# Rotations and squares of the last attention mixer on GpSimd, its values evacuated by VectorE, the exponential's table loaded early

## The chip, the cores and the metric

The program runs on one core of one Trainium2 chip. A core has TensorE (matrix products, called PE in the profile), VectorE (DVE), ScalarE (ACT), GpSimd (POOL) and SyncE (SP, which here only issues the transfers). Every engine works through its own list of instructions in order; semaphores tie the lists together. The metric is the time of one execution on the device in microseconds (us), and of several executions the median.

## What is computed

Two blocks of a transformer on 256 positions of width 1024, batch 1, all in float32. The first block has a recurrent layer, a sparse attention and a feed-forward part. The second has two layers, each with a feed-forward part, a mixer and another feed-forward part. The mixer of its second layer, the odd mixer, is what most of the change touches:

```python
proj = rmsnorm(x, od_norm) @ od_w_in
c_q, c_kv, k_pe, gq, gk, gv = split(proj)          # 256, 128, 32, 512, 128, 128 columns
q = (rmsnorm(c_q, od_cq_norm) @ od_w_uq)           # 8 heads of 64 + 32
kv = (rmsnorm(c_kv, od_ckv_norm) @ od_w_ukv)       # 8 heads of 64 (keys) + 64 (values)
k = concat(k_nope, k_pe for all heads)
q, k = rmsnorm(q), rmsnorm(k); the last 32 columns of a head are rotated (rope)
out_c = gqa_attention(q, k, v_c)                   # 8 heads, called D in the kernel
qd, kd = axial_rope(rmsnorm(gq)), axial_rope(rmsnorm(gk))
out_d = gqa_attention(qd, kd, gv)                  # 8 query heads on 2 key heads, called C
mix = concat(out_c, out_d) @ od_w_out;  x = x + mix
```

`gqa_attention` is softmax(q k / sqrt(d)) v.

## The kernel before

**Weights.** All weights stream once through the core, in chunks of 128x1024 float32 or less (`stream`, numbered). SyncE transfers chunk i into a ring of six buffers (`RAW`); ScalarE rounds it to the fast matmul format (`hi(e, i)`, line 312, result `WH`); VectorE computes what the rounding left over (`lo(e, i)`, line 318, result `WL`, which also frees the `RAW` buffer for SyncE). TensorE then adds three products per piece of 128 input features (lines 345 to 347): high activation by high weight, high by low, low by high. Activations are split in the same way, `AT0h`/`AT0l` for the layer's input and `AT3h`/`AT3l` for the latents of the odd mixer. `dense(e, p, x0, x1)` issues passes x0 to x1 of product p; a pass is one chunk for one half of the positions.

**The odd mixer** runs on the profile from about 1124 us to 1236 us. TensorE computes OGQ and OGK (queries, keys and values of attention C) and OCQ (the latents), turns keys and latents (transposes by a matmul with the identity, line 391), and computes UKV and UQ (keys, values and queries of attention D from the latents). Then come the eight units of attention C and the eight of D. A unit is two heads on 128 query positions:

- `pe_scores` writes the scores of unit u into PSUM bank 4 or 5 (`att_s`)
- `dve_max` takes their maxima (lines 538, 541)
- `act_exp` makes the exponentials and their sums (line 557, `att_e`), which frees the bank
- `pe_turn_p` turns them into bank 6 (line 391, `SR` or `SL`); it waits for `act_exp` of its unit and `act_p` of the unit before
- `act_p` copies the turned block out (line 599), and `pe_values` multiplies with the values (line 616)

After four units `dve_out`, `pe_turn_out`, `act_out_hi` and `dve_out_lo` prepare the input of the output product (OO for C, OP for D). Since TensorE takes its list in order, other work stands between the steps of the units: passes of UKV, UQ, OO and OP.

**Before the units** each product is evacuated by ScalarE: `act_ukv` (lines 1800, 1802, 1804: keys, their squares, values), `act_uq` (lines 1811, 1812: queries, their squares). VectorE rotates in six instructions per group (`dve_odd_rot`, lines 1660 to 1671, groups gq, gk, pe, q), sums the squares (`dve_mla_sums`, line 1703), takes the roots and scales the keys. ScalarE's table of functions has to hold the exponential before line 557; what is in use before (the SiLU set of the feed-forward part) does not have it, so a table load stands ahead of the first `act_exp`.

**The order** of all engines in the mixers is written out by hand, as lists (`pe_odd_mixer`, `act_odd_mixer`, `dve_odd_mixer` and the same for the first mixer and for the norm between its feed-forward part and the second block, `pe_post_norm`, `act_post_norm`, `dve_post_norm`). GpSimd has 21 instructions in the whole program, none of them in the odd mixer but one clearing of `KG`.

## Time and profile before

| | us |
|---|---|
| median of three executions | 1427.22 |
| lowest, highest | 1423.85, 1429.24 |
| the profiled execution | 1423.9 |
| its span, first to last instruction | 1422.1 |
| TensorE busy in it | 1393.8 (98%) |
| VectorE busy | 879.7 (62%) |
| ScalarE busy | 770.7 (54%) |
| GpSimd busy | 13.0 (1%) |

The profiled execution took 1.8 us more than its span. The page also gives the clock granted to TensorE: 0.994 on average, where 1.0 is 2.4 GHz and 0.5 is 1.2 GHz, the only two levels. Busy time of TensorE contains the pipelined tail of every matmul, about 0.17 us, so a wait shorter than that is invisible and a longer one looks that much shorter. Starts of instructions are the better ruler: in steady work a 128x512 matmul starts every 0.23 us.

### The profile page before, as it was taken

What the parts mean: (1) busy time and instruction counts of PE and PEld (TensorE: products, weight loads), DVE (VectorE), ACT (ScalarE), POOL (GpSimd) and SP (SyncE); (2) the same over time, 40 slices, a digit from 0 to 9 for tenths busy, and PEclk for the clock granted to TensorE, in tenths of its full rate; (3) what the DMA queues carried; (4) which work ended last, traced back from release to release, by engine and by line L of the source; (5) the groups of instructions that cost most, each with busy time, mean ns of one, the idle gap of its engine ahead of it and who ended that gap; (6) DMA issues with size and microseconds to landing.
All of it is one profiled execution on the core that took longest, in us unless ns stands there. A gap on an engine that the chain in (4) does not pass through costs nothing.

```text
span 1422.1 us, 18520 instructions
## 1 busy us (share of the span) xinstructions
PE 1393.8 (98%) x6978; PEld 1173.7 (83%) x6978; DVE 879.7 (62%) x1345; ACT 770.7 (54%) x1169; POOL 13.0 (1%) x21
## 2 busy tenths in 40 slices
PE   7999999999999999999999999999999989999999
PEld 6799888788887888888788888888888868888887
DVE  6889846665545755557976555565555674565543
ACT  5589844554545544445765444454444576554441
POOL 2000000000000000000000000000000000000000
PEclk9999999999999999999999999999999989999999
DMA  8453556476655566566346655666655431366651
GB/s 298 142 161 106 160 166 182 144 216 184 190 180 168 187 186 185 182 189 205 113 155 196 190 180 191 183 189 180 188 182 189 145 118 59 106 212 187 191 180 60
DMA packets 131767, 242.57 MB, mean 171 GB/s; under 512 B 8544, under 2 KB 21472, under 8 KB 131680
## 3 DMA queue, kind: packets, MB, share of 16 engines
q1 hardware_dynamic: 130768, 239.15, 54.7%
q0 software_dynamic: 624, 2.10, 0.5%
q8 instruction: 57, 0.93, 0.3%
q14 instruction: 30, 0.25, 0.0%
q10 hardware_dynamic: 288, 0.14, 0.0%
HBM read 240.31 MB, written 1.05 MB: 170 GB/s over the span
## 4 chain that ended last, share of the span: by engine, by line
PE 95%; DVE 2%; ACT 2%; issue 0%; DMA 0%; SPq 0%; ACTq 0%; DVEq 0%
PE PB L345 28%; PE PB L347 27%; PE PB L346 27%; PE PB L391 5%; PE PB L616 2%; PE PB L505 2%; PE PB L339 1%; PE PB L341 1%; PE PB L340 1%; DVE WL L318 1%; PE PB L509 0%; DMA X<-in_x_dram 0%; DVE XC L783 0%; PE PB L797 0%; PE PB L986 0%
## 5 line engine op out<-in xcount | busy, mean ns | idle before, releaser
L318 DVE TENSOR_TENSOR WL<-RAW,WH 128x1024 fp32r<-128x1024 f32 (+1 forms) x453 | 548.4, 1217 | 442.4 <-ACT WH L312 440.9
L312 ACT ACTIVATE WH<-RAW 128x1024 fp32r<-128x1024 f32 (+1 forms) x453 | 475.6, 1055 | 517.2 <-PE PB L347 509.0
L345 PE MATMUL PB<-WH,AT0h 128*128 128x512 f32 (+3 forms) x1328 | 507.9, 382 | 6.6 <-DVE AT0l L1232 6.5
L347 PE MATMUL PB<-WH,AT0l 128*128 128x512 f32 (+3 forms) x1328 | 497.6, 375 | 0.0
L346 PE MATMUL PB<-WL,AT0h 128*128 128x512 f32 (+3 forms) x1328 | 497.0, 374 | 0.0
L345 PEld LDWEIGHTS PB<-WH,AT0h 128*128 128x128 f32 x1328 | 250.9, 189 | 51.6 <-issue 10.1
L347 PEld LDWEIGHTS PB<-WH,AT0l 128*128 128x128 f32 x1328 | 250.7, 189 | 44.7
L346 PEld LDWEIGHTS PB<-WL,AT0h 128*128 128x128 f32 x1328 | 251.2, 189 | 44.1 <-issue 2.2
L345 PE MATMUL PB<-WH,FTh 128*128 128x512 f32 x440 | 172.1, 391 | 0.0
L347 PE MATMUL PB<-WH,FTl 128*128 128x512 f32 x440 | 171.3, 389 | 0.0
L346 PE MATMUL PB<-WL,FTh 128*128 128x512 f32 x440 | 171.2, 389 | 0.0
L347 PEld LDWEIGHTS PB<-WH,FTl 128*128 128x128 f32 x440 | 82.6, 188 | 17.3
L346 PEld LDWEIGHTS PB<-WL,FTh 128*128 128x128 f32 x440 | 82.7, 188 | 16.8
L345 PEld LDWEIGHTS PB<-WH,FTh 128*128 128x128 f32 x440 | 82.6, 188 | 16.8
L1280 ACT ACTIVATE SR<-PB,SM 128x512 f32<-128x512 f32 (+1 forms) x60 | 38.7, 653 | 24.7 <-PE PB L347 24.6
L391 PE MATMUL PB<-ID,SR 128*128 128x128 f32 x316 | 45.2, 277 | 5.2 <-ACT SR L557 5.0
L391 PEld LDWEIGHTS PB<-ID,SR 128*128 128x128 f32 x316 | 37.6, 144 | 12.3 <-ACT SR L557 5.5
L1309 ACT ACTIVATE FTh<-PB 128x512 fp32r<-128x512 f32 x55 | 30.2, 596 | 21.3 <-PE PB L391 21.3
L1287 DVE SCALAR_TENSOR_TENSOR SR<-PB,SM,SR 128x512 f32<-128x512 f32 (+1 forms) x60 | 39.9, 700 | 0.5
L339 PE MATMUL PB<-AT0h,WH 128*128 128x256 f32 x128 | 39.6, 309 | 0.0
L1315 DVE TENSOR_TENSOR FTl<-PB,FTh 128x512 fp32r<-128x512 f32 x55 | 35.6, 686 | 2.4 <-ACT FTh L1309 0.3
L341 PE MATMUL PB<-AT0h,WL 128*128 128x256 f32 x128 | 36.1, 282 | 0.0
(304 smaller groups left out, 1043.0 us busy)
## 6 DMA issues: line engine op xcount, KB each, us to landing
RAW<-in_ffn_w_gu_dram SPq DMA_DIRECT2D x88, 512.0 KB, 4.0
RAW<-in_ffn_w_gu_2b_dram SPq DMA_DIRECT2D x88, 512.0 KB, 3.7
RAW<-in_w_in_dram SPq DMA_DIRECT2D x48, 512.0 KB, 4.1
RAW<-in_ffn_w_down_dram SPq DMA_DIRECT2D x44, 512.0 KB, 3.3
RAW<-in_ffn_w_down_2b_dram SPq DMA_DIRECT2D x44, 512.0 KB, 3.3
RAW<-in_w_ffn_gate_dram SPq DMA_DIRECT2D x22, 512.0 KB, 4.0
RAW<-in_w_ffn_up_dram SPq DMA_DIRECT2D x22, 512.0 KB, 3.7
RAW<-in_w_ffn_down_dram SPq DMA_DIRECT2D x22, 512.0 KB, 3.6
```

What stands on the lines that cost most here:

```text
L312: e.activation(WH[i % NHL][:, 0:m], RAW[i % NRAW][:, 0:m], ACT.Copy).then_inc(*up("hi", i))
L318: e.tensor_tensor(WL[i % NHL][:, 0:m], RAW[i % NRAW][:, 0:m], WH[i % NHL][:, 0:m].bitcast(F32), ALU.subtract).then_inc(*up("lo", i))
L339: e.matmul(o, h[:, f], p.src[0][:, kx, :], start=start, stop=False, skip_group_check=True)
L341: ins = e.matmul(o, l[:, f], p.src[0][:, kx, :], start=False, stop=stop, skip_group_check=True)
L345: e.matmul(o, p.src[0][:, kx, t], h[:, j:j + p.n], start=start, stop=False)
L346: e.matmul(o, p.src[0][:, kx, t], l[:, j:j + p.n], start=False, stop=False)
L347: ins = e.matmul(o, p.src[1][:, kx, t], h[:, j:j + p.n], start=False, stop=stop)
L391: ins = e.transpose(PB[bank][0:s.shape[1], j * 128:j * 128 + 128], s, ID[:, :])
L1280: e.activation(silu_out(f, g, b), PB[p.banks[b]][:, 0:p.n], ACT.Silu, scale=RS[f"f{f}"][:, b:b + 1]).then_inc(*up("f_silu", (f, g, b)))
L1287: e.scalar_tensor_tensor(sl, PB[p.banks[b]][:, 0:p.n], RS[f"f{f}"][:, b:b + 1], sl, ALU.mult, ALU.mult).then_inc(*up("f_mult", (f, g, b)))
L1309: e.activation(FT[0][:, t:t + 2, :].rearrange("p t s -> p (t s)"), PB[4 + 2 * (g % 2) + q][:, :], ACT.Copy).then_inc(*up("f_hi", (f, g, q)))
L1315: e.tensor_tensor(FT[1][:, t:t + 2, :].rearrange("p t s -> p (t s)"), PB[4 + 2 * (g % 2) + q][:, :], FT[0][:, t:t + 2, :].rearrange("p t s ...
```

## The change

1. In the odd mixer the four rotations go from VectorE to GpSimd, 24 instructions (`pool_odd_rot`). They count on a semaphore of their own (`rot`).
2. The squares of keys and queries, eight instructions, go from ScalarE (out of PSUM) to GpSimd (out of the evacuated copies, `pool_uk_square`, `pool_uq_square`).
3. The values are evacuated by VectorE (`dve_uv`) instead of ScalarE, after ScalarE has read the same bank.
4. Of the squares of the latents, the second half of the positions goes from ScalarE to VectorE (`dve_cq_square`).
5. `act_warm`, one exponential of a 128x1 tile, stands behind the input of the odd mixer. The table load goes with it.
6. The lists of all engines are written in another order, in the odd mixer, in the first mixer and in the norm before the second block. Products, sizes and the stream of weights are the same.

```diff
@@ -1649,26 +1649,34 @@
                     "gk": [OUT3[:, :, 512 + z * 64:576 + z * 64].rearrange("p b (h d) -> p b h d", h=2) for z in range(2)],
                     "pe": [KT3[:, 2 * z:2 * z + 2, 0:16].unsqueeze(2) for z in range(2)]}
 
-        def dve_odd_rot(e, name, part):
+        def pool_odd_rot(e, name, part):
             x, h, half, tabs, i = ROT[name]
             x1, x2 = x[:, :, :, 0:half], x[:, :, :, half:2 * half]
             tmp = ROT_ROOM[name]
             tab = lambda j: tabs[:, i, j].unsqueeze(2).broadcast_to([128, 2, h, half])
             if part == 0:
                 e.wait_ge(*on(*ROT_FROM[name]))
-                e.wait_ge(*(on("heads", ("gq", 2)) if name == "q" else on("tab", "o")))
-                e.tensor_tensor(tmp[0], x1, tab(0), ALU.mult).then_inc(*up("dve"))
-                e.tensor_tensor(tmp[1], x2, tab(1), ALU.mult).then_inc(*up("heads", (name, 0)))
+                e.wait_ge(*(on("rot", ("gq", 2)) if name == "q" else on("tab", "o")))
+                e.tensor_tensor(tmp[0], x1, tab(0), ALU.mult).then_inc(*up("rot"))
+                e.tensor_tensor(tmp[1], x2, tab(1), ALU.mult).then_inc(*up("rot", (name, 0)))
             elif part == 1:
-                e.wait_ge(*on("heads", (name, 0)))
+                e.wait_ge(*on("rot", (name, 0)))
                 if name == "pe":
-                    e.wait_ge(*on("jk", ("cq", 1, 2)))
-                e.tensor_tensor(x1, x1, tab(2), ALU.mult).then_inc(*up("dve"))
-                e.tensor_tensor(x2, x2, tab(3), ALU.mult).then_inc(*up("heads", (name, 1)))
+                    e.wait_ge(*on("jk", ("cq", 2)))
+                    e.wait_ge(*on("cqs", 2))
+                e.tensor_tensor(x1, x1, tab(2), ALU.mult).then_inc(*up("rot"))
+                e.tensor_tensor(x2, x2, tab(3), ALU.mult).then_inc(*up("rot", (name, 1)))
             else:
-                e.wait_ge(*on("heads", (name, 1)))
-                e.tensor_tensor(x1, x1, tmp[1], ALU.subtract).then_inc(*up("dve"))
-                e.tensor_tensor(x2, x2, tmp[0], ALU.add).then_inc(*up("heads", (name, 2)))
+                e.wait_ge(*on("rot", (name, 1)))
+                e.tensor_tensor(x1, x1, tmp[1], ALU.subtract).then_inc(*up("rot"))
...
@@ -1698,12 +1706,13 @@
 
             v = v_m[:, 16 * i:16 * i + 16]
             v3 = v.rearrange("p (b h) -> p b h", b=2)
-            e.wait_ge(*on("evac", (("uks1", "uqs1")[i], 1)))
+            e.wait_ge(*on("usq", ("kq"[i], 1, 1)))
             sq = SQ3[:, :, 512 * i:512 + 768 * i].rearrange("p b (h d) -> p b h d", h=8)
             e.tensor_reduce(v3, sq, AXX, ALU.add).then_inc(*up("dve"))
             e.wait_ge(*last("dve"))
             if i == 0:
-                e.wait_ge(*on("jk", ("cq", 1, 2)))
+                e.wait_ge(*on("jk", ("cq", 2)))
+                e.wait_ge(*on("cqs", 2))
                 e.scalar_tensor_tensor(v3, v3, 96 * EPS, ssp.unsqueeze(2).broadcast_to([128, 2, 8]), ALU.add,
                                        ALU.add).then_inc(*up("heads", ("v", "k")))
             else:
...
+            q_ready=[("rot", ("q", 2))], k_ready=[("mkT", 3)], v_ready=[("uv", (1, 1))], q_first=1,
             bank6=[("att_p", ("c", 7))], bank45={0: [("att_e", ("c", 6))], 1: [("att_e", ("c", 7))]},
             bank7={0: [("o_lo", ("c", 1))], 1: [("o_lo", ("d", 0))]},
             slot_free={u: [("att_tp", ("c", u + 2))] for u in range(6)},
@@ -1778,15 +1787,26 @@
                 e.scalar_tensor_tensor(AT3[1][:, t, :], PB[6 + q][:, i * S:i * S + S], col("cq", t),
                                        AT3[0][:, t, :].bitcast(F32), ALU.mult, ALU.subtract).then_inc(*up("cq_lo", t))
 
-        def act_cq_square(e, b):
-            e.wait_ge(*on("evac", ("cq", b)))
+        CQ_PARTS = ((0, 256), (256, 128), (384, 32))
+
+        def act_cq_square(e):
+
+            e.wait_ge(*on("evac", ("cq", 0)))
             e.wait_ge(*last("jk"))
-            cond_square(e, JK[:, 0, 0:256], CQ[:, b, 0:256], ssc[:, b:b + 1], ("cq", b, 0))
-            cond_square(e, JK[:, 1, 0:128], CQ[:, b, 256:384], ssc[:, 2 + b:3 + b], ("cq", b, 1))
-            cond_square(e, JK[:, 1, 128:160], CQ[:, b, 384:416], ssp[:, b:b + 1], ("cq", b, 2))
+            for i, (o, n) in enumerate(CQ_PARTS):
+                t = (ssc[:, 0:1], ssc[:, 2:3], ssp[:, 0:1])[i]
+                cond_square(e, JK[:, 0, o:o + n], CQ[:, 0, o:o + n], t, ("cq", i))
+
+        def dve_cq_square(e):
+            e.wait_ge(*on("evac", ("cq", 1)))
+            for i, (o, n) in enumerate(CQ_PARTS):
+                x, t = CQ[:, 1, o:o + n], (ssc[:, 1:2], ssc[:, 3:4], ssp[:, 1:2])[i]
+                e.scalar_tensor_tensor(JK[:, 1, o:o + n], x, 1.0, x, ALU.mult, ALU.mult,
+                                       accum_out=t).then_inc(*up("cqs", i))
 
         def dve_cq_root(e):
-            e.wait_ge(*on("jk", ("cq", 1, 2)))
+            e.wait_ge(*on("jk", ("cq", 2)))
+            e.wait_ge(*on("cqs", 2))
             e.tensor_scalar(ssc[:, 0:2], ssc[:, 0:2], 0.5, 128 * EPS, ALU.mult, ALU.add).then_inc(*up("dve"))
             e.tensor_scalar(ssc[:, 2:4], ssc[:, 2:4], 128 * EPS, None, ALU.add).then_inc(*up("dve"))
...
@@ -1799,24 +1819,35 @@
             e.wait_ge(*on("rc", "rc"))
             e.activation(kh[:, b, 4 * c:4 * c + 4, 0:64], x[:, :, 0:64], ACT.Copy,
                          scale=s).then_inc(*up("evac", (f"uk{c}", b)))
-            e.activation(SQ3[:, b, c * 256:c * 256 + 256].rearrange("p (h d) -> p h d", d=64), x[:, :, 0:64], ACT.Square,
-                         scale=s).then_inc(*up("evac", (f"uks{c}", b)))
-            e.activation(V3[:, b, c * 256:c * 256 + 256].rearrange("p (h d) -> p h d", d=64), x[:, :, 64:128], ACT.Copy,
-                         scale=s).then_inc(*up("evac", (f"uv{c}", b)))
+        def dve_uv(e, c, b):
+            x = PB[UKV[c].banks[b]][:, :].rearrange("p (h d) -> p h d", d=128)
+            e.wait_ge(*on("evac", (f"uk{c}", b)))
+            e.tensor_scalar(V3[:, b, c * 256:c * 256 + 256].rearrange("p (h d) -> p h d", d=64), x[:, :, 64:128],
+                            ysc[:, 2 + b:3 + b], None, ALU.mult).then_inc(*up("uv", (c, b)))
+
+        def pool_uk_square(e, c, b):
+            x = kh[:, b, 4 * c:4 * c + 4, 0:64]
+            e.wait_ge(*on("evac", (f"uk{c}", b)))
+            e.tensor_tensor(SQ3[:, b, c * 256:c * 256 + 256].rearrange("p (h d) -> p h d", d=64), x, x,
+                            ALU.mult).then_inc(*up("usq", ("k", c, b)))
+
+        def pool_uq_square(e, c, b):
+            n = UQ[c].n
+            x = Q3[:, b, 512 * c:512 * c + n]
+            e.wait_ge(*on("evac", (f"uq{c}", b)))
+            e.tensor_tensor(SQ3[:, b, 512 + 512 * c:512 + 512 * c + n], x, x, ALU.mult).then_inc(*up("usq", ("q", c, b)))
 
         def act_uq(e, c, b):
             p, s = UQ[c], ysc[:, b:b + 1]
             x = PB[p.banks[b]][:, 0:p.n]
             e.wait_ge(*on("mm", p.end(b)))
             e.activation(Q3[:, b, 512 * c:512 * c + p.n], x, ACT.Copy, scale=s).then_inc(*up("evac", (f"uq{c}", b)))
-            e.activation(SQ3[:, b, 512 + 512 * c:512 + 512 * c + p.n], x, ACT.Square,
-                         scale=s).then_inc(*up("evac", (f"uqs{c}", b)))
...
@@ -2269,11 +2295,11 @@
             pe_scores(e, AT_C, 1)
             dense(e, UKV[1], 1, 2)
             dense(e, UQ[0], 0, 2)
-            dense(e, UQ[1], 0, 2)
             pe_turn_p(e, AT_C, 0)
             pe_scores(e, AT_C, 2)
+            dense(e, UQ[1], 0, 2)
+            pe_turn_p(e, AT_C, 1)
             pe_scores(e, AT_C, 3)
-            pe_turn_p(e, AT_C, 1)
             pe_values(e, AT_C, 0)
             pe_turn_q(e, AT_C, 1)
             pe_values(e, AT_C, 1)
@@ -2281,66 +2307,64 @@
             pe_scores(e, AT_C, 4)
             pe_scores(e, AT_C, 5)
             pe_turn_p(e, AT_C, 3)
+            pe_values(e, AT_C, 2)
+            pe_values(e, AT_C, 3)
+            pe_turn_p(e, AT_C, 4)
+            pe_scores(e, AT_C, 6)
+            pe_scores(e, AT_C, 7)
...
@@ -2678,6 +2702,7 @@
             hi(e, 371)
             act_x_hi(e, 'od', 2)
             act_x_hi(e, 'od', 3)
+            act_warm(e)
             hi(e, 372)
             hi(e, 373)
             act_gq(e, 0)
...
+            act_cq(e, 1)
             act_keys3(e, 0)
-            act_keys3(e, 1)
-            act_cq(e, 1)
-            act_cq_square(e, 0)
             act_cq_hi(e, 0)
             act_cq_hi(e, 1)
-            act_cq_square(e, 1)
+            act_keys3(e, 1)
+            hi(e, 380)
             act_q(e, AT_C, 0)
-            hi(e, 380)
             hi(e, 381)
             act_ukv(e, 0, 0)
             act_ukv(e, 0, 1)
             act_ukv(e, 1, 0)
             act_ukv(e, 1, 1)
+            hi(e, 382)
+            act_exp(e, AT_C, 0)
             act_uq(e, 0, 0)
             act_uq(e, 0, 1)
-            act_uq(e, 1, 0)
-            act_uq(e, 1, 1)
-            act_exp(e, AT_C, 0)
             act_exp(e, AT_C, 1)
             act_p(e, AT_C, 0)
-            hi(e, 382)
+            act_uq(e, 1, 0)
             hi(e, 383)
+            act_uq(e, 1, 1)
+            act_exp(e, AT_C, 2)
             act_p(e, AT_C, 1)
-            act_exp(e, AT_C, 2)
+            act_exp(e, AT_C, 3)
             act_q(e, AT_C, 1)
-            act_exp(e, AT_C, 3)
+            hi(e, 384)
             act_p(e, AT_C, 2)
-            hi(e, 384)
...
@@ -2780,31 +2804,31 @@
         def dve_first_mixer(e):
             lo(e, 0)
             lo(e, 1)
+            lo(e, 2)
             dve_in_lo(e, 0)
             dve_in_lo(e, 1)
             dve_in_lo(e, 2)
-            dve_in_lo(e, 3)
-            lo(e, 2)
             lo(e, 3)
             lo(e, 4)
+            dve_in_lo(e, 3)
             lo(e, 5)
...
-            dve_post_root(e, 'f1', 1)
+            lo(e, 143)
             dve_block_lo(e, 'f1', 0, 0)
             dve_block_lo(e, 'f1', 0, 1)
+            dve_post_root(e, 'f1', 1)
+            lo(e, 144)
             dve_post(e, 'f1', 1, 0)
             dve_post(e, 'f1', 1, 1)
-            lo(e, 143)
-            lo(e, 144)
             dve_block_lo(e, 'f1', 1, 0)
+            dve_rs(e, 'f1')
             dve_block_lo(e, 'f1', 1, 1)
-            dve_rs(e, 'f1')
...
             lo(e, 374)
-            dve_odd_rot(e, 'gq', 2)
             lo(e, 375)
-            dve_odd_rot(e, 'gk', 0)
             dve_gqa_sums(e)
-            dve_odd_rot(e, 'gk', 1)
+            lo(e, 376)
             dve_gqa_root(e)
-            dve_odd_rot(e, 'gk', 2)
-            lo(e, 376)
-            dve_gqa_keys(e)
             lo(e, 377)
             lo(e, 378)
+            dve_gqa_keys(e)
             lo(e, 379)
-            dve_odd_rot(e, 'pe', 0)
+            dve_cq_square(e)
             dve_cq_lo(e, 0)
             dve_cq_lo(e, 1)
             dve_cq_root(e)
-            dve_odd_rot(e, 'pe', 1)
+            lo(e, 380)
+            dve_uv(e, 0, 0)
+            dve_uv(e, 0, 1)
+            dve_uv(e, 1, 0)
             dve_max(e, AT_C, 0)
+            dve_uv(e, 1, 1)
             dve_max(e, AT_C, 1)
-            lo(e, 380)
-            dve_odd_rot(e, 'pe', 2)
+            dve_mla_sums(e, 0)
             lo(e, 381)
-            dve_mla_sums(e, 0)
-            dve_odd_rot(e, 'q', 0)
+            dve_max(e, AT_C, 2)
+            lo(e, 382)
+            dve_max(e, AT_C, 3)
             dve_mla_sums(e, 1)
...
@@ -3185,6 +3202,28 @@
             lo(e, 393)
             lo(e, 394)
             lo(e, 395)
...
```

The order at three places. The first is VectorE at the start of the program: `GR` is the normed input, line 444 makes `AT0l`, which the first product waits for.

```order
 L422 TENSOR_SCALAR GR<-X,SM 128x512 x4
-L318 TENSOR_TENSOR WL<-RAW,WH 128x1024 x2
-L444 SCALAR_TENSOR_TENSOR AT0l<-PB,CO,AT0h 128x256 x8
-L318 TENSOR_TENSOR WL<-RAW,WH 128x1024 x2
+L318 TENSOR_TENSOR WL<-RAW,WH 128x1024 x3
+L444 SCALAR_TENSOR_TENSOR AT0l<-PB,CO,AT0h 128x256 x6
+L318 TENSOR_TENSOR WL<-RAW,WH 128x1024
 L318 TENSOR_TENSOR WL<-RAW,WH 128x576
+L444 SCALAR_TENSOR_TENSOR AT0l<-PB,CO,AT0h 128x256 x2
 L318 TENSOR_TENSOR WL<-RAW,WH 128x1024
```

A third weight chunk now stands ahead of the first `AT0l`. The second place is VectorE in the norm before the second block, where lines 359 to 376 with 128x1 operands are the root of the second half of the positions.

```order
 L1195 TENSOR_TENSOR X<-SR,X 128x512
-L318 TENSOR_TENSOR WL<-RAW,WH 128x1024
+L318 TENSOR_TENSOR WL<-RAW,WH 128x1024 x2
+L1232 SCALAR_TENSOR_TENSOR AT0l<-PB,CO,AT0h 128x128 x8
 L1181 SCALAR_TENSOR_TENSOR SM<-SM 128x1
 L359 TENSOR_SCALAR SM<-SM 128x1
```

The eight instructions that make `AT0l` moved ahead of that root, and one more weight chunk ahead of them. The third place is ScalarE in the odd mixer, from the last squares of the keys to the second unit of attention C, first of before:

```order
L1804 ACTIVATE V<-PB,SM 128x256
L1811 ACTIVATE Q<-PB,SM 128x512
L1812 ACTIVATE SQ<-PB,SM 128x512
L1811 ACTIVATE Q<-PB,SM 128x512
L1812 ACTIVATE SQ<-PB,SM 128x512
L1811 ACTIVATE Q<-PB,SM 128x256
L1812 ACTIVATE SQ<-PB,SM 128x256
L1811 ACTIVATE Q<-PB,SM 128x256
L1812 ACTIVATE SQ<-PB,SM 128x256
L557 ACT_TABLE_LOAD
L557 ACTIVATE SR,SM<-PB,SM 128x256 x4
```

and of the change, from the keys on (line 1820 is `act_ukv`, 1844 is `act_uq`):

```order
L1820 ACTIVATE K<-PB,SM 128x4x64 x4
L312 ACTIVATE WH<-RAW 128x1024
L557 ACTIVATE SR,SM<-PB,SM 128x256 x2
L1844 ACTIVATE Q<-PB,SM 128x512 x2
L557 ACTIVATE SR,SM<-PB,SM 128x256 x2
L599 ACTIVATE PT<-PB 128x512
L1844 ACTIVATE Q<-PB,SM 128x256
L312 ACTIVATE WH<-RAW 128x1024
L1844 ACTIVATE Q<-PB,SM 128x256
```

The first exponential moved ahead of all evacuations of the queries; squares, values and the table load are gone from between. The table load now stands behind line 1250 at the mixer's start; the number of table loads in the program is 21 in both.

## Rows read from the trace of the kernel before

**Rows 1.** The page's first part: busy time, share of the span, instructions.
```profile
PE 1393.8 (98%) x6978; PEld 1173.7 (83%) x6978; DVE 879.7 (62%) x1345; ACT 770.7 (54%) x1169; POOL 13.0 (1%) x21
```
**Rows 2.** Waits of PE in the whole span: total us, times, longest.
```profile
PE PB L391 <- ACT SR L557: 5.0, 2, 4.4
```
**Rows 3.** Busy us of each engine, PEclk, DMA by window; window and length first.
```profile
75.00:180.00 105.00, 104.86 (x704) 94.38 (x702) 89.85 (x147) 89.40 (x181) 1.26 (x3) 1.00 0.46 139
1147.00:1161.00 14.00, 12.31 (x54) 9.32 (x52) 9.23 (x29) 12.94 (x37) 0.00 (x0) 0.88 0.45 146
1161.00:1170.00 9.00, 4.65 (x10) 2.36 (x10) 5.72 (x17) 7.97 (x17) 0.00 (x0) 0.68 0.21 63
1170.00:1188.00 18.00, 16.59 (x120) 13.98 (x120) 11.75 (x21) 14.48 (x38) 0.00 (x0) 0.97 0.28 87
1188.00:1224.00 36.00, 36.00 (x226) 31.77 (x225) 15.57 (x28) 21.49 (x52) 0.00 (x0) 1.00 0.20 60
```
**Rows 4.** Timeline of PE, odd mixer: start, duration, line, tiles, count, idle before.
```profile
1165.47 1.11 PE L391 MATMUL PB<-ID,SR 128*128 128x128 f32 x4 [4.35 <-ACT SR L557]
...
1169.79 1.06 PE L391 MATMUL PB<-ID,SR 128*128 128x128 f32 x4
...
1178.41 0.61 PE L391 MATMUL PB<-ID,SL 128*128 128x128 f32 x4
1178.86 1.00 PE L616 MATMUL PB<-G,PT 128*128 128x64 f32 x8
1179.70 1.08 PE L505 MATMUL PB<-KG,QT 128*128 128x512 f32 x2
1180.61 0.60 PE L391 MATMUL PB<-ID,SL 128*128 128x128 f32 x4
...
1192.73 0.58 PE L345 MATMUL PB<-WH,AT0h 128*128 128x512 f32 x1
```
**Rows 5.** Timeline of ACT, odd mixer.
```profile
1153.69 1.06 ACT L312 ACTIVATE WH<-RAW 128x1024 fp32r<-128x1024 f32 x1 [1.04 <-PE PB L347]
1154.65 0.46 ACT L1800 ACTIVATE K<-PB,SM 128x256 f32<-128x256 f32 x1
...
1155.36 0.47 ACT L1804 ACTIVATE V<-PB,SM 128x256 f32<-128x256 f32 x1
...
1158.93 0.77 ACT L1811 ACTIVATE Q<-PB,SM 128x512 f32<-128x512 f32 x1
1159.50 0.78 ACT L1812 ACTIVATE SQ<-PB,SM 128x512 f32<-128x512 f32 x1
...
1162.92 1.28 ACT L557 ACT_TABLE_LOAD   x1
1164.21 0.56 ACT L557 ACTIVATE SR<-PB,SM 128x256 f32<-128x256 f32 x1
...
1165.31 0.56 ACT L557 ACTIVATE SR<-PB,SM 128x256 f32<-128x256 f32 x1
```
**Rows 6.** Groups of DVE by form, 1130 to 1188 us: busy us, mean ns.
```profile
L1703 DVE TENSOR_REDUCE SM<-SQ 128x16 f32<-128x1536 f32 x1 | 1.7, 1747 | 0.0
...
L1660 DVE TENSOR_TENSOR OUT<-G,TG 128x512 f32<-128x512 f32 x1 | 0.7, 691 | 1.4 <-ACT G L1633 1.4
```
**Rows 7.** Groups of POOL by form, whole span: busy us, mean ns.
```profile
L648 POOL MEMSET IKT<- 128x512 f32 x1 | 0.5, 544 | 0.0
...
L1018 POOL TENSOR_SCALAR_AFFINE_SELECT SC<-SC 128x256 f32<-128x256 f32 x1 | 0.4, 408 | 7.3 <-DVE SC L1012 7.3
```
**Rows 8.** Timelines of DVE and PE at the start of the program.
```profile
11.16 2.35 DVE L318 TENSOR_TENSOR WL<-RAW,WH 128x1024 fp32r<-128x1024 f32 x2
13.43 3.22 DVE L444 SCALAR_TENSOR_TENSOR AT0l<-PB,CO,AT0h 128x256 fp32r<-128x256 f32 x8
...
14.05 0.47 PE L345 MATMUL PB<-WH,AT0h 128*128 128x512 f32 x1
```
**Rows 9.** Timelines of DVE and PE in the norm before the second block.
```profile
461.61 2.15 DVE L1232 SCALAR_TENSOR_TENSOR AT0l<-PB,CO,AT0h 128x128 fp32r<-128x128 f32 x8
...
462.87 0.47 PE L345 MATMUL PB<-WH,AT0h 128*128 128x512 f32 x1 [3.25 <-DVE AT0l L1232]
```

450 lines of the change are left out of this document (229 added, 221 removed).

## The prediction, made before the changed kernel ran

> **What bounds the kernel now.** I read the page's first part, then PE's waits, then the windows of the odd mixer, then the timelines there. TensorE is busy for 98% of the span [rows 1], so only what keeps it standing or at its lower clock can be given back. Its longest wait outside the start is for the first exponentials of attention C, 5.0 us in two waits, one of 4.4 [rows 2]. The windows show where the loss lies [rows 3]. From 1147 to 1188 us TensorE is not busy for 14 - 12.31 = 1.69, 9 - 4.65 = 4.35 and 18 - 16.59 = 1.41 us, together 7.45. The granted clock there is 0.88, 0.68 and 0.97, and since time at the lower level (1.2 GHz) does half the work, that is another 0.12 x 14 + 0.32 x 9 + 0.03 x 18 = 1.7 + 2.9 + 0.5 = 5.1 us. So about 12.5 us is all that the odd mixer has to give. Behind it, from 1188 to 1224, TensorE is busy in 36.00 of 36 us at full clock, and in the first mixer's dense part (75 to 180) in 104.86 of 105 us: there a new order can gain nothing and can only lose.
>
> **The ScalarE chain of the odd mixer (parts 2, 3 and 5 of the change).** Before, ScalarE runs from the first key evacuation at 1154.65 to the table load at 1162.92 without a gap. Keys, squares, values of one block take 0.36 us each (0.71 for two, 1154.65 to 1155.36), a 512 wide query block or its squares 0.57 (1158.93 to 1159.50). Then come 1.28 us of table load, and the exponentials start at 1164.21, one unit each 1.10 us (1164.21 to 1165.31) [rows 5]. TensorE turns unit 0 at 1165.47 and unit 1 at 1169.79, the latter at the lower clock [rows 4].
>
> Afterwards, walked with the same durations: the fourth key evacuation still has to wait for the last UKV pass, and ends near 1157.0. One weight chunk follows (about 1.0 us, the step from 1153.69 to 1154.65 in [rows 5]), so the exponentials of unit 0 run from 1157.9 to 1159.0. TensorE has finished the UQ[0] passes at 1159.1 and turns unit 0 at once, computes the scores of unit 2 (0.91, from 1179.70 to 1180.61) and the two UQ[1] passes (1.4), and can turn unit 1 at 1161.9; the exponentials of unit 1 end at 1161.2. That is 7.9 us ahead of 1169.79, with one scores unit less behind it: 7.0 ahead. The table load costs nothing where it goes: ScalarE is waiting for TensorE there, for about as long as the load, and the next weight chunk is needed many passes later. If that cover failed it would cost at most its 1.28 us.
>
> **What is late next.** The rest of attention C. ScalarE has per unit 1.10 us of exponentials and 0.5 of copy, TensorE 0.45 (turn), 0.84 (values) and 0.91 (scores) [rows 4]. Three short waits remain in my walk: 1.1 us where the second query turn waits for the copy of unit 1, 0.3 for that query copy, 0.7 where the exponentials of unit 4 wait for VectorE, which has the sums of the query squares (1.75 us, [rows 6]) and the root ahead of its maxima: 2.1 in all. Ahead of them the latents' chain keeps 1.3 us of its 1.69 idle, and the clock drop behind it 1.6. So 12.5 - 2.1 - 2.9 = 7.5 us are given back. A second count agrees roughly: continued to the scores of attention D, the walk puts TensorE 8.1 us ahead of where it is at 1192.73. I take **7.5 us**, with 4 and 11 as ends. Attention D keeps enough passes of OO and OP between its steps to stay full, as it is now [rows 3].
>
> **The latents (part 4).** One set of three small squares leaves ScalarE's path between the second latent evacuation and `AT3h`, and key evacuations take most of its place: 0.4 us, contained in the 7.5. It cannot exceed the 1.69 us.
>
> **GpSimd (parts 1 and 2).** The trace shows no GpSimd instruction with two inputs. The floor is the clearing of 128x512, 0.54 us; one input for 256 elements costs 0.41, so 0.82 for 512, and two inputs read in turn would be 1.64 [rows 7]. I take the middle of the last two, 1.2 us per 512, against 0.69 on VectorE [rows 6]. The rotation of the queries (6 x 1.2) and of the keys (6 x 0.3) then runs from 1133.0 to 1142.0, and the key product has to be ready at 1146.9, with 0.4 us for VectorE between. So these 9 us lie beside TensorE's OGK and OCQ passes. They stay covered up to about 1.58 us per 512; at the end of 1.64 they cost 0.4. The squares of the queries end at about 1164.1 and gate the sums named above; at 1.64 they cost about 0.9. The rotation of the D queries ends near 1168, and is needed near 1182. Nobody else waits in GpSimd's queue: its transfers are all issued earlier.
>
> The rotations' own time on VectorE disappears, but VectorE was not what TensorE waited for, so that gain is nought. The values cost VectorE four instructions of 128x256 in place of it, and the banks of UQ now come free through it; it has them done by 1157.4, before TensorE needs the second bank.
>
> The Trainium skill (GPSIMD Engine Reference, section 3.1) has GpSimd's `tensor_tensor` 1.96 times slower than VectorE's. By that, as an estimate, a 512 wide one takes 1.35 us; no run here shows it yet, and the sum would stay the same, since 1.35 is below 1.58.
>
> **The start (part 6).** VectorE now makes a third low weight chunk ahead of the first `AT0l`. Two take from 11.16 to 13.43, so one is 1.14 us; its input is ready in time. `AT0l` starts at 13.43 and TensorE's first product at 14.05 [rows 8], and TensorE has no wait of length until far behind. So the start is **1.1 us later**, with nothing to take it up; between 0.5 and 1.2, since TensorE's transposes end near 14.0 too.
>
> **The norm before the second block (part 6).** TensorE stands for 3.25 us there; `AT0l` starts at 461.61 and the product at 462.87 [rows 9], behind one weight chunk and the eight small instructions of a root. After the change two weight chunks stand ahead (1.14 more) and the root (1.65) does not: **0.5 us earlier**, between 0 and 0.8. The root then falls behind `AT0l`, under four dense passes of 1.36 us.
>
> **The first mixer (part 6).** The order moves between products, none of which is added. With 0.14 us idle in 105 it can gain nothing there; what a slip costs is a wait of the kind this trace has, 0 to 3 us. I take 0.
>
> **Sum.** -7.5 - 0.5 + 1.1 = **-6.9 us** against the profiled execution of 1423.9 (span 1422.1), so 1417.0. That execution lies 3.3 us below the median of 1427.2; the median moves by the same amount, to **1420.3**.
>
> **The rivals.**
> A, the forecast: 4.5 to 9 us gained, 1418.2 to 1422.7. Chance 0.50.
> B, the walk is too careful: the clock does not drop behind the latents, and the short waits vanish, worth up to 1.6 + 2.1, so 9 to 11 us gained, about 1417. For it: the idle stretches there become shorter. Against it: the latents' chain keeps most of its links. Chance 0.13.
> C, the clock drops once more: TensorE gets short waits, 2.1 us within 8, where before it had one long one, and a drop like the one around 1166 to 1170 costs 1.7 to 3. Gain about 4.5, 1422.7. Against it: from 1170 to 1188 it had 1.41 us of waits and stayed near 0.97. Chance 0.14.
> D, the first mixer slips: 3 us lost where VectorE and ScalarE are each busy for 89 of 105 us [rows 3]. Gain about 4, 1423.4. Chance 0.13.
> E, slower than before: GpSimd's two-input instructions are far slower than the rows suggest, and `pe_keys3` stands in TensorE's order ahead of the whole chain. Per us above 1.58 for 512 elements the two rotations end 6 x 1.25 = 7.5 us later and TensorE stands as long, and the squares add some 3 us at the sums. Above 2.3 us the gain of 6.9 is gone; at 3 us the time is 1434. The end of the rows is 1.64, which speaks against it. Chance 0.07.
> F, VectorE and GpSimd hinder one another. The Trainium skill (SBUF — State Buffer, "Who interferes with whom") says that a VectorE instruction with two SBUF inputs and a GpSimd one that reads SBUF exclude each other for the whole instruction. No row here shows it. As a mechanism of this kernel: the weight chunk ahead of the maxima of units 2 and 3 and the root are such instructions, and GpSimd has its squares and rotations at that time; each could be held for one GpSimd instruction, 0.6 to 1.2 us, two or three of them in the path. Gain about 5, 1422.3. Chance 0.03 on its own, since A's lower end holds most of it.
>
> **How the numbers follow.** The likeliest case is A, so 1420.3. B's end and the spread of the medians (1423.9 to 1429.2 before) put the low end at 1415.5; C, D, F and a median 2 us off put the high end at 1426; E is left out. What a measurement can tell from no change is about 0.5%, here 7.1 us, to 1420.1. The forecast of 6.9 lies on that bound. Faster: half of A less a little (0.23), all of B and some of the rest by the medians' spread (0.20), 0.43. Slower by over 0.5%: the worse part of E and chance, 0.06. Within 0.5%: 0.51.
>
> **What would show it.** The table load near 1126 us and none at the first exponentials; PE's wait of 4.35 us for `SR` gone, the exponentials of unit 0 near 1158, unit 1 turned near 1162; the first product at 15.1 instead of 14.05; the wait in the norm near 2.7 instead of 3.25; GpSimd's 128x512 instruction between 0.8 and 1.6 us, and no wait of PE at line 391 for the keys. It would be wrong if a wait of several us stood in the first mixer, if PEclk fell to 0.5 a second time between 1160 and 1185, or if GpSimd's squares ended long after 1164 and the maxima of unit 4 with them.

## The result, and the profile after

| | before | changed |
|---|---|---|
| median, us (20 executions each, same chip) | 1428.82 | 1422.78 |
| lowest, highest | 1423.85, 1429.53 | 1419.16, 1424.21 |
| ratio, 95% interval | | 0.9965 [0.9956, 0.9973] |
| span of the profiled execution | 1422.1 | 1421.0 |

By the ratio, in which all kernels are compared, the change gains 5.0 us (3.9 to 6.3), within the 0.5% that was called no change; the two medians differ by 6.0. Forecast were 6.9 us and 1420.3; the range holds the time.

The two profiled spans differ by only 1.1 us, the medians by more. That of before is its shortest execution (1423.9 where the median of 20 is 1428.8). Most executions of before have a mean granted clock between 0.990 and 0.993 (15 of 18 beside the first experiments), this one had 0.994. So one trace against one trace tells where waits are, and not what the clock costs on average. I keep the two apart below.

TensorE's waits over 0.15 us in the changed kernel (us in total, times, longest), against [rows 2]:

```profile
PE PB L391 <- DVE GR L422: 10.6, 1, 10.6
PE PB L345 <- DVE AT0l L1232: 6.0, 2, 3.2
PE PB L391 <- ACT SL L557: 2.3, 1, 2.3
PE PB L391 <- POOL CQ L1671: 1.3, 1, 1.3
PE PB L345 <- DVE AT0l L444: 0.9, 1, 0.9
PE PB L391 <- ACT PT L599: 0.9, 1, 0.9
PE PB L391 <- DVE G L1702: 0.5, 1, 0.5
PE PB L391 <- ACT QT L487: 0.2, 1, 0.2
```

The wait of 4.4 for `SR` is gone; of the last six, five stand in the odd mixer. (`CQ L1671` is the latents' pause. TensorE waits there to turn the queries into the bank from which `AT3h` and `AT3l` are made; the profile names GpSimd's rotation, which ended at nearly the same moment. In the kernel's list this step waits for the first `AT3l`, which ended at 1155.86, 0.15 us before TensorE's start; in rot_on_vector below, without rotations on GpSimd, the profile names `AT3l` here.) The windows of [rows 3] in the changed kernel. This execution reached the odd mixer 5.6 us later than that of before (GpSimd clears `KG` at 1126.1 instead of 1120.5), so each shows work that lies 5.6 us earlier:

```profile
1147.00:1161.00 14.00, 12.16 (x63) 10.10 (x63) 12.76 (x38) 9.82 (x22) 6.89 (x15) 1.00 0.42 151
1161.00:1170.00 9.00, 8.07 (x47) 6.24 (x46) 8.81 (x15) 8.84 (x22) 6.96 (x8) 1.00 0.39 122
1170.00:1188.00 18.00, 15.47 (x96) 12.31 (x95) 13.39 (x26) 12.21 (x32) 4.94 (x6) 1.00 0.30 87
```

TensorE is not busy for 1.84 + 0.93 + 2.53 = 5.30 us (before 7.45), and the granted clock, which cost 5.1 us there, is 1.00 throughout. Together 12.5 became 5.3: the odd mixer gained 7.2 us in this pair of executions, the sum as forecast (7.5), but 2.15 of it by waits and 5.1 by the clock, where I had 4.05 and 3.5. Some 0.6 us of the 12.5 is counted twice: the clock was already low before the wait for `SR` ended, and in a wait it costs nothing. The window of that wait in before (0.13 x 4.4 = 0.6):

```profile
1161.00:1165.40 4.40, 0.12 (x1) 0.00 (x0) 2.80 (x5) 4.37 (x11) 0.00 (x0) 0.87 0.43 129
```

The ScalarE chain went as walked. ScalarE, then TensorE, of the changed kernel:

```profile
1131.22 1.28 ACT L1679 ACT_TABLE_LOAD   x1
...
1162.47 0.56 ACT L557 ACTIVATE SR<-PB,SM 128x256 f32<-128x256 f32 x1
...
1164.69 0.59 ACT L557 ACTIVATE SR<-PB,SM 128x256 f32<-128x256 f32 x1
...
1163.72 0.66 PE L391 MATMUL PB<-ID,SR 128*128 128x128 f32 x4
...
1166.55 0.63 PE L391 MATMUL PB<-ID,SR 128*128 128x128 f32 x4
...
1178.38 0.66 PE L391 MATMUL PB<-ID,SL 128*128 128x128 f32 x4 [2.30 <-ACT SL L557]
```

Less the 5.6 us, the exponentials of unit 0 start at 1156.9 (forecast 1157.9), unit 0 is turned at 1158.1 (1159.1) and unit 1 at 1160.9 (1161.9). The load of 1.28 us delays nobody. What was not forecast is the last row, 2.30 us where I had 0.7.

Where the loss went, the three stretches ahead. The start, TensorE of the changed kernel:

```profile
15.18 0.77 PE L345 MATMUL PB<-WH,AT0h 128*128 128x512 f32 x1 [0.95 <-DVE AT0l L444]
15.75 0.63 PE L346 MATMUL PB<-WL,AT0h 128*128 128x512 f32 x1
16.18 0.63 PE L347 MATMUL PB<-WH,AT0l 128*128 128x512 f32 x1
...
19.59 0.49 PE L346 MATMUL PB<-WL,AT0h 128*128 128x512 f32 x1
```

```profile
466.88 0.72 PE L345 MATMUL PB<-WH,AT0h 128*128 128x512 f32 x1 [2.74 <-DVE AT0l L1232]
```
```profile
465.00:470.00 5.00, 3.12 (x8) 2.47 (x9) 4.64 (x18) 2.76 (x10) 0.00 (x0) 0.69 0.67 210
```
```profile
465.00:470.00 5.00, 5.00 (x27) 4.16 (x26) 4.77 (x11) 3.07 (x12) 0.00 (x0) 1.00 0.38 110
```

That is 0.31 x 5 = 1.5 us up to 470, and 1.7 with what lies behind (0.83 from 465 to 475). The norm before it, whose order is untouched, has the same wait of 3.25 us in both, and lost 1.7 us by the clock before and 3.4 after. The balance of the two profiled executions is then +1.1 and +2.1 (start), +1.7 (first norm), -0.5 and +1.7 (second norm), -7.2 (odd mixer), -1.1 together; the spans differ by -1.1. That it closes so well is in part chance: the 7.2 is 0.6 too large, and the 1.7 of the first norm 0.5, since there too more of the lower clock fell into the wait than in before.

And GpSimd. Its rotation of C's queries, VectorE beside it, then the same at the root over the squares:

```profile
1138.61 1.29 POOL L1660 TENSOR_TENSOR OUT<-G,TG 128x512 f32<-128x512 f32 x1 [11.56 <-ACT G L1633]
1139.87 1.28 POOL L1661 TENSOR_TENSOR OUT<-G,TG 128x512 f32<-128x512 f32 x1
1141.22 1.95 POOL L1667 TENSOR_TENSOR G<-G,TG 128x512 f32<-128x512 f32 x1
1143.14 1.74 POOL L1668 TENSOR_TENSOR G<-G,TG 128x512 f32<-128x512 f32 x1
...
1139.93 3.80 DVE L318 TENSOR_TENSOR WL<-RAW,WH 128x832 fp32r<-128x832 f32 x2 [2.79 <-ACT WH L312]
...
1171.78 1.79 POOL L1668 TENSOR_TENSOR Q<-Q,TM 128x256 f32<-128x256 f32 x1
1173.64 0.77 POOL L1671 TENSOR_TENSOR Q<-Q,OUT 128x256 f32<-128x256 f32 x1
...
1171.76 1.21 DVE L318 TENSOR_TENSOR WL<-RAW,WH 128x1024 fp32r<-128x1024 f32 x1
1172.89 0.70 DVE L359 TENSOR_SCALAR SM<-SM 128x32 int32<-128x32 int32 x1
1173.63 0.18 DVE L361 TENSOR_SCALAR SM<-SM 128x32 int32<-128x32 int32 x1
1173.85 0.61 DVE L367 TENSOR_TENSOR SM<-SM 128x32 f32<-128x32 f32 x1
```

GpSimd takes 1.28 us alone (forecast 1.2), and up to 1.95 where VectorE splits a chunk; the two chunks take 3.80 us, where one of this size took 1.02 in before. At 1171.76 VectorE's chunk and GpSimd's `L1668` start together: GpSimd's takes 1.79 instead of 0.73, that is, it ends 0.6 us after the chunk. `L359`, 0.17 us in before, starts at 1172.89 and ends with it, at 1173.6; `L361` starts with `L1671`, in the gap, and takes 0.18; `L367` starts behind the start of `L1671` and ends late again, 0.61 where it took 0.19. The pattern is one of turns, not of sharing.

### The profile page after: what moved, and what is told of

The parts are those of the page before. It is cut to its first block, busy times and chain, and to the rows that moved or that the text cites. A ratio compares the mean times of both kernels' runs of the same rounds, so it can differ in the third digit from the quotient of the medians.

```text
span 1421.0 us, 18521 instructions
## 1 busy us (share of the span) xinstructions
PE 1394.6 (98%) x6978; PEld 1174.8 (83%) x6978; DVE 881.5 (62%) x1331; ACT 765.3 (54%) x1152; POOL 40.2 (3%) x53
## 4 chain that ended last, share of the span: by engine, by line
PE 94%; DVE 4%; ACT 1%; issue 0%; DMA 0%; SPq 0%; DVEq 0%; ACTq 0%
PE PB L345 28%; PE PB L347 27%; PE PB L346 27%; PE PB L391 5%; PE PB L616 2%; DVE WL L318 1%; PE PB L505 1%; PE PB L339 1%; PE PB L340 1%; PE PB L341 1%; PE PB L509 0%; PE PB L797 0%; DMA X<-in_x_dram 0%; PE PB L986 0%; DVE SM L538 0%
```

## The experiments

All times are ratios to the kernel before on the same chip. Each interval is some 0.25 to 0.4% wide, 4 to 6 us, so waits are read from the traces and the ratios only bear on larger effects. "Clock" is what a lower granted clock cost: (1 - granted clock) x the length of a window that is narrow around the stretch. In a window of 60 us the two digits are good to 0.3 us only: before reads 0.91 there, 5.4 us, where [rows 3] give 5.1.

### What the parts of the change do

**odd_alone**: the three lists of the first mixer and the three of the norm as before, the rest as changed.

> The changed kernel with the lists of the first mixer and of the norm before the second block as before: the odd mixer's change alone. Theory T (the sum by stages of the two traces holds: the odd mixer gained 7.4 us, the rest of the change lost it back): 7.4 us below before, a ratio of 0.9948, and about 2.4 us below the changed kernel. Rival R (the 2.9 us of lower clock behind the latents went away by the luck of where this stage begins, and not by the shorter wait): it comes back here, since the stage begins 3 us earlier than in the changed kernel; about 5 us below before, 0.9965, with a granted clock below 0.95 between the latents and the scores of unit 2.

Measured: 1421.44, ratio 0.9965 [0.9953, 0.9977], 5.0 us gained (3.3 to 6.7). The waits of the odd mixer are those of the changed kernel (5.30 us not busy, clock 0). T's 7.4 lies outside the interval. R's 5 lies inside, but its mark, a low clock between the latents and unit 2, is absent in the one trace: neither theory holds as it was written. The odd mixer alone gives the whole gain within the interval, and the gain is near 5, not 7.4.

**rest_alone**: the kernel before with those six lists of the change.

> The kernel before with only the new lists of the first mixer and of the norm before the second block. Theory T: the start costs 3.2 us (1.1 of a third low weight chunk, 2.1 of the ten matmuls that then run at a start every 0.43 instead of 0.23 us), the norm between -0.5 and +1: 2.7 to 4.2 us above before, ratio 1.0019 to 1.0029. Rival R (the start costs the 1.1 us of the chunk and nothing else; the rest of the difference was one execution's scatter): 0.6 to 1 us above before, 1.0005.

Measured: 1425.79, ratio 0.9994 [0.9982, 1.0007]: from 2.6 us gained to 1.0 lost. T's 2.7 to 4.2 us of loss are excluded, R's 0.6 to 1 is not. The trace says why. The first product starts at 15.05 after a wait of 1.04, as in the changed kernel, but the next matmuls start 0.23 us apart at once:

```profile
15.05 0.47 PE L345 MATMUL PB<-WH,AT0h 128*128 128x512 f32 x1 [1.04 <-DVE AT0l L444]
15.36 0.40 PE L346 MATMUL PB<-WL,AT0h 128*128 128x512 f32 x1
```

So the wait of 1.1 us belongs to the order, and the ten slow matmuls are no fixed part of it.

**start_old**: VectorE's third chunk behind `AT0l` again.

```diff
             lo(e, 1)
-            lo(e, 2)
             dve_in_lo(e, 0)
...
+            dve_in_lo(e, 3)
+            lo(e, 2)
```

> The changed kernel with VectorE's order at the start as before: the third low weight chunk behind the four parts of AT0l; nothing else. Theory T: 3.2 us below the changed kernel, 8 us below before, ratio 0.9943; TensorE's first product at 14.05 with starts 0.23 us apart from the second on, where the changed kernel has 0.43 for ten of them. Rival R: only the chunk's 1.1 us, 6 us below before, 0.9957.

Measured: 1421.55, ratio 0.9962 [0.9950, 0.9974]. R's 0.9957 lies inside, T's 0.9943 outside. The wait ahead of the first product is gone, but some matmuls behind it run at the low pace (0.5 us in all). Over the profiles of this study that loss at the first products was 2.1, 2.3 and 0 us with the new order and between 0 and 1.3 with the old one (eleven profiles). Whether the longer wait makes it larger stays open; three profiles are too few.

**norm_old**: the changed kernel with the norm's lists of before.

> The changed kernel with the lists of the norm before the second block as before. Theory T (the new order gains the 0.5 us of wait that it seems to gain, and the lower clock behind it, 0.69 against 1.00, came from the moment at which the wait fell, not from the order): the time differs from the changed kernel by less than 1.5 us, and the granted clock behind the wait may be at either level; with the low level the wait is 3.25 and the time 0.5 us above the changed kernel. Rival R (the new order itself brings the lower clock): 1.2 us below the changed kernel, at 1.00 behind the wait.

Measured: 1422.15, ratio 0.9969 [0.9958, 0.9980] beside 0.9965 for the changed kernel. The wait is 3.25 again, and the lower clock behind it is there too (0.89 from 460 to 475, 1.7 us). So T holds: the order gains its 0.5 us of wait, and the clock there is not its doing.

**load_alone**: `act_warm` and its call, in the kernel before.

> The kernel before with the one exponential of 128x1 behind the odd mixer's input and nothing else, so that the table is loaded there. Theory T: the load of 1.28 us leaves ScalarE's chain, TensorE's wait at SR falls from 4.35 to 3.1, and the time by 1.3 us (0.9991) with the granted clock behind that wait as before, 0.50 to 0.68; the other 6 us of the odd mixer's gain come from the order and from squares and values that left ScalarE. Rival J (the table load is the main part of the gain, since a shorter wait also keeps the clock): 4 us, 0.9972, with a granted clock near 1 behind the wait.

Measured: 1426.30, ratio 0.9989 [0.9976, 1.0001]. The wait and the window:

```profile
PE PB L391 <- ACT SR L557: 4.1, 2, 3.4
```
```profile
1140.00:1200.00 60.00, 53.60 (x309) 44.72 (x308) 41.02 (x101) 45.27 (x117) 0.00 (x0) 0.94 0.31 97
```

The longest wait falls by 1.0 us and the clock behind it still falls; J's 0.9972 is outside the interval. T's 0.9991 is inside. The early table load is worth about 1 us of the 5. Which part of the rest belongs to the squares, to the values or to the new order of the lists, no run separates.

### The clock behind the waits

**before_again**: the kernel before, profiled a second time.

> The kernel before, unchanged, in one more profiled execution. Theory T2 (the waits of a kernel are the same to 0.1 us in every execution, and what differs is behind which of them the granted clock falls to the lower level): the waits read 3.25, 3.25, 4.35 again, while the stretches at a start every 0.43 us lie elsewhere or are more of them; their difference makes the difference of the spans. Rival: the waits themselves differ by more than 0.5 us.

Measured: one execution of 1429.5, span 1427.7, 5.6 us longer than the first, with the same waits: 3.25, 3.25, 4.30, 0.70, 0.99. In the first 80 us the clock cost 3.4 instead of 1.7 us, behind the first norm's wait 3.4 instead of 1.7, behind the second's 1.7 instead of 0, and in the odd mixer 5.1 both times. These make 5.1 us; the low pace of the first products, which lies ahead of the clock's record, is another 1.1. Together 6.2, 0.6 more than the spans differ, in part because a lower clock costs nothing as long as a wait lasts. So T2 holds: one program, the same waits, and another clock behind them.

All fourteen profiles of the study, by the longest wait of TensorE in the stretch and whether a lower clock stood behind it:

| wait | profiles with a lower clock behind it | cost |
|---|---|---|
| odd mixer, 3.4 to 4.8 us for `SR` (before, before_again, rest_alone, load_alone, both_engines) | 5 of 5 | 3.4 |
| the latents of the same five, 0.70 and 0.99 us | 2 of 5 (before, before_again) | 1.7 |
| first norm, 3.25 us | 11 of 14 | 1.7 or 3.4 |
| second norm, 3.25 us | 4 of 6 | 1.7, once 3.4 |
| second norm, 2.74 us | 6 of 8 | 1.7 |
| odd mixer, 2.30 us for `SL` (changed, odd_alone, norm_old, start_old) | 1 of 4 | 3.4 |
| odd mixer, at most 1.3 us (the five kernels below) | 0 of 5 | 0 |
| from 28 to 37 us, no wait (during or just behind 48 matmuls that are 72 columns wide) | 12 of 14 | 1.7 or 3.4 |

So a long wait is not the only thing that a lower clock follows: it came twice behind two waits under 1 us, and in 12 profiles it came near 30 us, where TensorE had not stood still.

The windows of 60 us of three of these: before_again, start_old (the one of four), both_moved.

```profile
1140.00:1200.00 60.00, 52.63 (x300) 43.87 (x299) 41.95 (x101) 44.61 (x110) 0.00 (x0) 0.91 0.31 98
```
```profile
1140.00:1200.00 60.00, 54.68 (x316) 45.28 (x315) 41.60 (x91) 41.06 (x100) 20.36 (x28) 0.94 0.27 87
```
```profile
1140.00:1200.00 60.00, 55.60 (x338) 46.47 (x337) 42.15 (x94) 43.83 (x110) 20.27 (x28) 1.00 0.27 87
```

In the odd mixer the clock cost (5.1 + 5.1 + 3.4 + 3.4) / 4 = 4.3 us on average with the lists of before (without load_alone), and 3.4 / 4 = 0.9 with those of the change: 3.4 us gained. With the 2.15 us of waits that is 5.6, less the 0.6 net of start and norm 5.0, which is what was measured. That is an estimate from four profiles against four, and the 0.9 hangs on one of them: the agreement to 0.1 us is luck. The mean granted clock of all executions points the same way: 0.9918 over 18 of before, 0.9946 over 20 of the changed kernel, and 0.0028 x 1425 = 4.0 us.

### GpSimd against VectorE

**both_engines**: the kernel before, GpSimd set to work in a feed-forward part (at 946 us, in place of the 880 that I had expected).

```diff
+            for n in range(3):
+                e.wait_ge(*last("zero"))
+                for o in outs:
+                    e.tensor_tensor(o, PT3[:, 0, :], PT3[:, 1, :], ALU.mult).then_inc(*up("zero"))
+            for n in range(2):
+                e.wait_ge(*last("zero"))
+                for o in outs:
+                    e.tensor_scalar(o, PT3[:, 0, :], 2.0, None, ALU.mult).then_inc(*up("zero"))
```

> The kernel before, with 24 multiplications of two SBUF inputs of 128x512 and then 16 multiplications by a constant (one input) put on GpSimd in the feed-forward part at about 880 us, where VectorE splits weight chunks (two SBUF inputs, 1.13 us each) and evacuates PSUM. Theory F (VectorE and GpSimd exclude each other for whole instructions): a two-input instruction of GpSimd takes 1.28 us alone, and 1.28 plus what is left of VectorE's instruction where one runs, up to 2.4; VectorE's weight chunk takes up to 1.28 more than 1.13. Nothing waits for GpSimd, so the time hardly moves, unless VectorE becomes late for TensorE. Rival K (they share the port's time in halves, or only GpSimd is slowed): VectorE's instructions keep their durations, or all are stretched in proportion to the overlap and none is held ahead of its start. For one input I have no expectation but that it is not slower than two.

Groups of VectorE by form from 946 to 991 us, busy us and mean ns, of both_engines and then of before; after that one of the three groups of GpSimd's 24 (the other two have 1930 and 1941 ns):

```profile
L318 DVE TENSOR_TENSOR WL<-RAW,WH 128x1024 fp32r<-128x1024 f32 x16 | 28.9, 1803 | 13.7 <-ACT WH L312 13.7
L1287 DVE SCALAR_TENSOR_TENSOR SR<-PB,SM,SR 128x512 f32<-128x512 f32 x4 | 2.8, 738 | 0.0
```
```profile
L318 DVE TENSOR_TENSOR WL<-RAW,WH 128x1024 fp32r<-128x1024 f32 x16 | 19.6, 1226 | 20.4 <-ACT WH L312 20.4
L1287 DVE SCALAR_TENSOR_TENSOR SR<-PB,SM,SR 128x512 f32<-128x512 f32 x4 | 2.8, 742 | 0.0
```
```profile
L1619 POOL TENSOR_TENSOR SQ<-PT 128x512 f32<-128x512 f32 x12 | 22.0, 1861 | 0.0
```

VectorE's chunk of two SBUF inputs goes from 1.23 to 1.80 us on average, the instructions that read PSUM stay at 0.74. GpSimd's 24 take 1.28 alone and 1.87 here. Of 45 us, GpSimd's work alone would take 24 x 1.28 = 30.7 and the 16 chunks 16 x 1.14 = 18.2, together 48.9: as long as if they had run one after the other, less what the ends overlap. Chunk by chunk it is the same: a chunk that starts 0.61 us behind a GpSimd instruction, which then has 0.68 us left, takes 1.77 us (at 947.35), one that starts 0.07 behind, with 1.22 left, takes 2.30 (at 967.56), and all 16 are longer than 1.23 us by what is left less 0.15. F holds and K falls. TensorE had one wait of 0.56 us by it.

The Trainium skill (SBUF — State Buffer, "Who interferes with whom") calls it an exclusive lock between VectorE instructions with two SBUF inputs and GpSimd ones that read SBUF, and says that VectorE's reductions never take part. The trace agrees: the reduction over the squares, 1.75 us in before, takes 1.75 in the changed kernel at 1169.65, with GpSimd's rotation beside it. For GpSimd instructions with one input the trace differs from an exclusion over the whole instruction; it is told at the end.

**rot_after_root**: start_old, with `e.wait_ge(*on("heads", "ym"))` ahead of GpSimd's rotation of the D queries.

> start_old with one wait more: GpSimd begins its rotation of the D queries only when VectorE's root over the squares (32 values) is done. Nothing is added or left out. Theory F (VectorE and GpSimd exclude each other for whole instructions, and this stretched the root from 2.0 to 3.3 us): the root takes 2.0 us again, GpSimd's fourth instruction 0.73 instead of 1.79, the maxima of unit 4 come 1.3 us earlier and TensorE's wait at SL falls from 2.30 to 1.0; 1.3 us below start_old. Rival G (the root is slow because of its own 32 values and the semaphores of a fuller program): the root stays at 3.3, the wait at 2.30, and the time is the same.

VectorE's root, GpSimd's rotation behind it, and TensorE's wait:

```profile
1169.67 0.17 DVE L359 TENSOR_SCALAR SM<-SM 128x32 int32<-128x32 int32 x1
...
1174.05 1.17 DVE L1731 TENSOR_TENSOR K<-CQ,SM 128x512 f32<-128x512 f32 x1
1175.14 1.75 DVE L1732 TENSOR_TENSOR K<-K,SM 128x1024 f32<-128x1024 f32 x1
...
1171.75 0.73 POOL L1660 TENSOR_TENSOR OUT<-Q,TM 128x256 f32<-128x256 f32 x1 [5.11 <-DVE SM L376]
```
```profile
PE PB L391 <- ACT SL L557: 0.7, 1, 0.7
```

F holds: the root takes 1169.67 to 1171.58, 1.9 us instead of 3.3, and the wait falls from 2.30 to 0.69. But now the keys' scaling pays: 1.17 and 1.75 us, where they took 0.68 and 1.22. Ratio 0.9945 [0.9927, 0.9963]. At `SL` it gains 1.6 us against start_old, and a wait of 0.34 us at `AT0l` is new.

**max_first**: start_old with `dve_max` of units 4 and 5 ahead of `dve_mla_root`.

> start_old with the maxima of units 4 and 5 ahead of the root on VectorE; the rotation stays where it is. Theory F: the wait of 2.30 at SL disappears, the root and the scaled keys come 1.7 us later, and TensorE stands about 1.2 us at the keys' transposes (line 391 from K) instead; net 1.1 us below start_old. Rival H (it is ScalarE that is late, and the maxima only seem to be the end of the chain): the wait at SL stays above 1 us.

Measured: ratio 0.9945 [0.9925, 0.9965]. No wait at `SL` is left, and 0.41 us at `K` and 0.33 at `AT0l` stand instead, less than the 1.2 expected. ScalarE was not the late one; H falls.

**both_moved**: both edits.

> start_old with both edits, the rotation behind the root and the maxima of units 4 and 5 ahead of it. Theory F: the root takes 2.0 us, no wait at SL and none above 0.3 us at the keys: 2.0 to 2.3 us below start_old, about 7.5 us below before, 0.9947. Rival H: as start_old, within 0.5 us. If the lower clock after a wait is what makes most of the difference between kernels, the gain is larger by up to 2 us, since no wait above 1.5 us is left between the latents and attention D.

Measured: 1417.86, ratio 0.9942 [0.9921, 0.9962]. No wait at `SL`, but 0.55 at `K` and 0.84 at `AT0l`, since the rotation now falls on the keys' scaling: 4.40 us not busy in the window, more than with either edit alone (4.04 and 3.76). The ratio is what F forecast (0.9947), the waits are half a miss, and by F's own mechanism: what is moved away from one VectorE instruction lands on the next.

**walk_again**: both_moved with GpSimd's rotation behind the scaled keys, and

```diff
             act_cq(e, 0)
-            act_cq_square(e)
             act_cq(e, 1)
-            act_keys3(e, 0)
             act_cq_hi(e, 0)
             act_cq_hi(e, 1)
+            act_cq_square(e)
+            act_keys3(e, 0)
```

and on VectorE the keys of C ahead of two chunks and `AT3l` ahead of its squares.

> both_moved with three more moves in the odd mixer: GpSimd's rotation of the D queries behind the scaled keys instead of behind the root; ScalarE evacuates the latents' second half, then makes AT3h, and only then the squares and the key copies; VectorE scales the keys of attention C ahead of two weight chunks and makes AT3l ahead of its squares. Theory F: the scaled keys take 1.22 instead of 1.76 us and TensorE's waits at K (0.55) and at OO's AT0l (0.84) fall to 0.3 together; the waits at the keys (0.52) and for the latents (1.32) fall to 1.1 together: 1.8 us below both_moved. Rival L (the key copies behind the latents are late for the first scores, or the clock's fall behind the waits decides): no gain, within 1 us of both_moved.

Measured: 1420.63, ratio 0.9946 [0.9929, 0.9964]. The waits at the keys and at `K` are gone, the latents' is 0.74, `AT0l`'s 0.37; a new one of 1.09 us stands at the first scores, for the query copy `QT` that ScalarE now makes after the key copies. Not busy: 3.29 us against 4.40. The waits gained 1.1 of the 1.8 us, the time did not show it. L's first half was right.

**rot_on_vector**: both_moved with the rotations in VectorE's list, none on GpSimd.

> both_moved with all four rotations back on VectorE, in gaps of its list (of C's queries and keys where before had them, of the latents' 32 columns behind the root, of the D queries behind the low half of OO's first input); the squares stay on GpSimd. It undoes part 1 of the change in the best order so far. Theory F (on GpSimd a rotation is 1.9 times as long and holds VectorE up besides, so that it takes from VectorE nearly what it saves): the root over 20 values takes 2.0 instead of 4.2 us, TensorE's wait for the keys of C is gone but the latents' is longer by as much, the waits at K and at OO's input stay within 0.5 us of both_moved's 0.55 and 0.84; the time is both_moved's within 1 us. Rival M (the rotations off VectorE are part of the gain): 2.3 us more of VectorE between 1160 and 1182 put the keys or the maxima that late; 1.5 to 2.5 us above both_moved, with the waits at K or SL that much longer.

Measured: 1420.52, ratio 0.9954 [0.9938, 0.9970]. TensorE's waits in the odd mixer:

```profile
PE PB L391 <- DVE AT3l L1787: 1.1, 1, 1.1
PE PB L391 <- ACT PT L599: 0.9, 1, 0.9
PE PB L391 <- DVE K L1732: 0.9, 1, 0.9
PE PB L391 <- ACT CQ L1640: 0.5, 1, 0.5
PE PB L345 <- DVE AT0l L1537: 0.3, 1, 0.3
```

The root over 20 values takes 2.1 us again, and TensorE is not busy for 3.94 us, where both_moved has 4.40. The ratio is 1.7 us worse, inside both intervals. By the waits F holds: with this order, the 24 instructions of the rotations on GpSimd buy nothing over VectorE. By time alone M is not excluded.

## Why the forecast came out as it did

- **Where the odd mixer's loss lies** (12.5 us in waits and clock): right, and it became 5.3 in the profiled execution. odd_alone shows it as the whole of the gain.
- **The ScalarE chain, the table load**: right to 1.0 us; load_alone puts the load by itself at 1.0 us of wait.
- **Where 12.5 us were to be had**: some 0.6 us of them were not, since the lower clock began before the wait for `SR` ended.
- **The latents**: I had 1.3 us of idle left and 0.4 gained. Measured 0.51 + 1.32 = 1.83, nothing gained. One part is the keys, which VectorE had late: its root over 20 values took from 1146.73 to 1151.03, 4.3 us, against 2.1 in before and in rot_on_vector. The other is my placement of two key copies ahead of `AT3h`; walk_again, which turns that round and also moves ScalarE's and VectorE's squares behind, has 0.74; the two moves are not separated.
- **The rest of attention C**: 2.1 us of short waits forecast, 0.93 + 0.23 + 2.30 = 3.5 measured. The step that failed is "0.7 where the exponentials of unit 4 wait for VectorE". I had priced the sums and the root by their durations in before. Held up by GpSimd the root takes 1.4 us more (1172.89 to 1176.21 against 1.9), and the small instruction ahead of it 0.2; rot_after_root gives 1.6 back. This is rival F, which I gave 0.03 as a case of its own. The mechanism and one of its places, the root, were named, and its price was inside A's range. The other place was not held: the two weight chunks ahead of the maxima of units 2 and 3 took 1.21 us each, as in before, and it was a later chunk, at 1171.76, that held GpSimd's rotation and so the root. The rule should have gone into the walk, as what is left of a GpSimd instruction for each VectorE one that it meets.
- **GpSimd's durations**: 1.2 us taken, 1.28 measured alone. "Covered from 1133.0 to 1142.0", 9 us, became 12.2 (1138.61 to 1150.77), since three of the six queries' instructions were held by VectorE (1.95, 1.74 and 1.74 us). "Covered up to 1.58" was a bound on GpSimd's work alone, and the cover failed by 0.5 us at an average of 1.55 for 512. The rotation ended at 1150.77; VectorE's root until 1151.03 and its two chunks until 1152.76 stood between that and the keys.
- **The clock**: "1.6 remain behind the latents" was wrong. Behind the latents it cost nothing in all nine profiles with the new lists, and with those of before 1.7 us in only two of five. Nor is it a constant of the kernel: behind the same waits it cost 0 in the changed kernel and 3.4 in start_old. I had read 5.1 us from one execution as if it were the kernel's own. On average the change gives back 3.4 us of it (four profiles against four), close to the 3.5 that I had, by luck of two errors: 0.9 us comes back behind the latents too, and 0.9 goes behind `SL`.
- **The start**: +1.1 is right as a delay (15.18, forecast 15.15). That its pace then falls was not in the forecast; it is not a fixed cost either (rest_alone).
- **The norm**: the wait of 2.74 as forecast; norm_old shows that the clock behind it is not the order's.
- **The first mixer at nought**: right, 105.00 us busy in 105 from 75 to 180, and no new wait.
- **The sum**: -6.9 forecast, -5.0 measured by the ratio. 1.9 us of waits are the difference (5.30 not busy where the walk left 3.4), and the clock's share came out even. By the medians it is -6.0; since that of before was also 1.6 us higher in 20 executions than in the three shown, the time landed 2.5 us above the forecast. The chance of 0.51 for no change was on the right side; the largest single reason is F, 1.6 us.

The five later orders can't be told apart by time, and hardly from the changed kernel (0.9942 to 0.9954 against 0.9965, with overlapping intervals). By TensorE's time not busy the best is walk_again, 3.29 us against 5.30.

## What to carry to other kernels

Work moved to GpSimd is not free for VectorE: in a walk, every VectorE instruction with two SBUF inputs, and small ones from SBUF to SBUF too, that meets a GpSimd instruction with two inputs is charged what is left of that one, and a long GpSimd stretch is placed where VectorE reads PSUM, reduces, or rests. The waits of TensorE from 2.7 us up cost more than themselves here, since the lower clock followed 26 of 33 of them; cutting one of 4.4 to 2.3 us gave back more than the 2 us of wait. And the clock's loss is read over several executions, never as a term of one trace.

## What the runs showed of the hardware

- Two-input multiplications of 128x512 float32 take GpSimd 1.28 us, and of 128x256 0.73; VectorE takes 0.69 and 0.42.
- With one input and a constant GpSimd was not quicker: 1.49 us at its quickest, 2.48 at its slowest over the 16 of both_engines. I have no explanation for it being slower than two inputs.
- Nor did these hold VectorE for their whole length. The seven chunks that started 0.67 us or more behind the start of one took 1.23 us, as alone, and the three within 0.2 us of it 1.49 to 1.51. GpSimd's instruction, then VectorE's chunk that starts inside it:

```profile
1015.79 1.49 POOL L1623 TENSOR_SCALAR SQ<-PT 128x512 f32<-128x512 f32 x1
```
```profile
1016.49 1.23 DVE L318 TENSOR_TENSOR WL<-RAW,WH 128x1024 fp32r<-128x1024 f32 x1 [2.01 <-ACT WH L312]
```

